# Dilated attention scores as two rounded 128-row products instead of one f32 product of 64 rows

## The chip, the cores and the metric

One core of one Trainium2 chip runs the whole program. Time is device microseconds of one execution; the figure for the kernel before is the median of three. The profile is of one further execution, and its times count from the start of its span.

## What is computed

Two transformer blocks over 512 tokens of width 1024, one after the other. The change is in the first block, in its dilated attention, cut here to what matters:

```python
def dilated_branch(q, k, v, rel_bias, window, dilation):
    ...
    s = jnp.einsum('bdhcqe,bdhcke->bdhcqk', qb, kb).astype(f32) + bias[:, None]
    s = jnp.where(mask, s, NEG)
    m = jnp.max(s, axis=-1, keepdims=True)
    p = jnp.exp(s - m)
    den = jnp.sum(p, axis=-1, keepdims=True)
    o = jnp.einsum('bdhcqk,bdhcke->bdhcqe', p, vb.astype(f32)) / den
    ...

def dilated_mixer(q, k, v, rel_bias):
    q = q * DSA_DH ** -0.5
    ...
    w = jax.nn.softmax(jnp.stack(lses, axis=0), axis=0)
    return jnp.sum(w[..., None] * jnp.stack(outs, axis=0), axis=0)

def first_block(x, ...):
    ...
    o_b = dilated_mixer(...).reshape(B, S, DSA_WIDTH)
    mixed = jnp.concatenate([o_a, o_b], axis=-1).astype(h.dtype)
    h = h + jnp.einsum('bsm,md->bsd', mixed, w_out[l])
```

There are 8 heads of 64 channels. The kernel folds the three dilations into one score matrix per head, with a table of biases (`toep`) that also counts how many dilations see a key, so each head needs one 512 x 512 causal score matrix.

## The kernel before, in words

Every large product is made of three rounded (fp32r) products: rounded part times rounded part, rest times rounded part, rounded part times rest. The three lines are L660, L664 and L667 (function `products`); a group of the three over 128 rows and 512 columns is called a triple below. The weights stream in on two DMA queues: SP loads raw pieces (`weights`, L2285), ScalarE rounds them (L1030) and writes the negated rounded part (L1038), and GpSimd's queue loads the same piece again, added onto that (L2187).

Each engine has one instruction list, written before the run by `merge`: every stream yields a due time before each step, and the step with the smallest due time is issued next. Due times set the order only; on the chip an engine runs its list in order and waits on semaphores. `T_A1` is the due time at which the product `wo0` (the first half of the output projection) starts, `R1` the due time between two steps of the dilated attention.

The dilated attention (`attention("dil", ...)` on TensorE, `dilated` on ScalarE and VectorE) runs in 12 steps beside the triples of `wo0`. A step s is a pair of heads `hp` (two heads, in partitions 0 to 63 and 64 to 127 of the pages `qD[hp]` and `kD[hp]`) and some rows of the score matrix; `ORDER` gives a pair three steps, of 384 columns, of 128 and 256 columns, and of 512 columns. One step goes through the engines like this:

- TensorE: the scores of both heads into banks `FB[0]` and `FB[1]`, in f32 with 64 rows per head (L858). This is called block S(s) below.
- VectorE: adds the bias and takes the row extreme (L1706), called the mask step; it frees the score bank for block S(s + 1).
- ScalarE: exponential with the row sum (L1152). VectorE: reciprocal (L1688) and scaling (L1693).
- TensorE, in step s + 2: transposes into `FB[2]`, `FB[3]` (L846), called T(s). ScalarE copies them out to `pT` (L1164).
- TensorE, in step s + 3: the values (L833), called AV(s), into bank `OB`. After a pair's third step VectorE copies `OB` out (L1676), which the next AV waits for.

```python
ORDER = [(hp, rows) for hp in range(4) for rows in (((2, 0),), ((0, 0), (1, P)), ((3, 0),))]
...
for i, at_ in rows_:
    n = (i + 1) * P
    for p in range(2):
        mm = e.matmul(FB[p][:, at_:at_ + n], qs[64 * p:64 * p + 64, hp, i * P:(i + 1) * P],
                      ks[64 * p:64 * p + 64, hp, 0:n], start=True, stop=True)
```

VectorE also adds finished tiles of `wo0` to the residual (L1755), and both engines split finished rows of `mixed` into rounded part (L1145) and rest (L1669).

Of the kernel before, what the change touches and what calls it, by code (L numbers as in the profile page):

```python
# [8 lines left out]
F32 = mybir.dt.float32  # L9
F32R = mybir.dt.float32r  # L10
U8 = mybir.dt.uint8
ALU = mybir.AluOpType
ACT = mybir.ActivationFunctionType

P = 128
# [255 lines left out]
def lo(x, k):  # L271
    return "operand_low", x, k
# [12 lines left out]
def build_program(nc, A, out):  # L285
    with ExitStack() as ctx:
# [20 lines left out]
        def rounded(name, n):  # L307

            return [nc.alloc_sbuf_tensor_at(f"{name}{i}_r", [P, S], F32R, offset=places[f"{name}{i}"])[:, :] for i in range(n)]
# [92 lines left out]
        AH2, AL2, ft2 = AH1_last, AL1_last, ft1  # L402
        sums2 = nc.alloc_sbuf_tensor_at("sums2", [P, 4 * UC], F32, offset=places["sq0"])[:, :]

        sq_r, gt_r, zb_r, eb_r = rounded("sq", 2), rounded("gT", 2), rounded("zb", 2), rounded("eb", 2)

        raw_r = nc.alloc_sbuf_tensor_at("RAW0_r", [P, 2 * S], F32R, offset=places["RAW0"])[:, :]
# [29 lines left out]
        def x_in(k):  # L437

            return [(f"x{k}",)]
# [5 lines left out]
        def freed(t):  # L445
            return ("evac_s" if t.st in on_act else "evac_v", t.g)
# [71 lines left out]
        def dil_done(hp):  # L518

            return T_A1 + R1 * (3 * hp + 5) + 0.9 if hp == 3 else T_A1 + R1 * (3 * hp + 6) + 1.3  # L520

        def row_stat(s, i, p):

# [92 lines left out]
        def tensor():  # L616
# [200 lines left out]
            def attention(name, T, R, q, apart, qs, ks, vs, zbuf, wbuf, q_key, k_key, v_keys, fence):  # L817
                for s in range(NA + 3):
# [29 lines left out]
                    if s < NA:  # L848
                        yield T + R * s + (2 * q if apart else q)
                        hp, rows_ = ORDER[s]  # L850
                        for p in range(2):
                            pe.wait_ge(q_key(hp), k_key(hp))
                            if s:
                                pe.wait_ge((name + "_b", s - 1, p))
# [5 lines that stand above are left out]
                                if (i, at_) == rows_[-1]:  # L860
                                    mm.then_inc(*pe.sig(name + "_z", s, p))
# [119 lines left out]
        def scalar():  # L981
# [160 lines left out]
            def mixed_split(st, k, time, waits):  # L1142
                yield time
                act.wait_ge(*waits)
                e.activation(NH[:, k, :], (mixed if st == "mixed" else mixed2)[:, k, :], ACT.Copy).then_inc(*act.sig(*hi(st, k)))  # L1145

            def exponentials(s):
                for p in range(2):
                    act.wait_ge(("dil_b", s, p))
                    for i, at_ in ORDER[s][1]:  # L1150
                        z, x = zs[2 * (s % 2) + p][:, at_:at_ + (i + 1) * P], row_stat(s, i, p)
                        ex = e.activation(z, z, ACT.Exp, scale=-1.0, bias=x[:, 0:1], accum_out=x[:, 2:3])  # L1152
                ex.then_inc(*act.sig("dil_e", s))
# [241 lines left out]
                return [up(t) if t.i % 2 else gate(t) for t in plan.stage["gu", g]]  # L1395

            streams = [prologue(), ones(), splits(), negated(), root("attn", mean_time["attn"]), columns("attn", 30.0)]
            streams += [natural("vG", vG, "attn"), natural("vD", vD, "attn")]
            streams += silu_gates("gG", lambda i: mixed[:, i, :], gt_, lambda i: [("gate", "gG", i - 2)] if i >= 2 else [])
            streams += [gla(0), gla(1)]  # L1400
            streams += [mixed_split("mixed", k, T_A1 - 2.0 + 0.2 * k, [("gla_out", k), ("product", "block", plan.last_unit("vD"), k)])
# [43 lines left out]
        def vector():  # L1445
# [220 lines left out]
            def mixed_split(st, k, time, waits):  # L1666
                yield time + 0.05
                dve.wait_ge(hi(st, k), *waits)
                e.tensor_tensor(NL[:, k, :], (mixed if st == "mixed" else mixed2)[:, k, :], NH[:, k, :].bitcast(F32),  # L1669
                                ALU.subtract).then_inc(*dve.sig(*lo(st, k)))  # L1670

            def heads_out(name, s, dst, last):
                hp = ORDER[s][0]
# [466 lines left out]
            streams += silu_gate("gG", lambda i: mixed[:, i, :], lambda i: g_gla[:, i:i + 1], gt_, [])  # L2140
            streams += [gla(0), gla(1), put("qD", qD, -0.125), put("kD", kD)]
            streams += [mixed_split("mixed", k, T_A1 - 2.0 + 0.2 * k, []) for k in range(4)]
            streams += [dilated(), to_h("wo0", "wo0", lambda k: x_in(k)[-1])]
            streams += [mixed_split("mixed", k, dil_done(k - 4), []) for k in range(4, 8)]
            streams += [to_h("wo1", "mlp", lambda k: ("h", "wo0", k)), sums("mlp")]
            streams += [operand_row("mlp", "n_mlp", k, square_time("mlp", k), g_mlp, [("h", "mlp", k)]) for k in range(4)]
# [118 lines left out]
        def sync():  # L2265
# [36 lines left out]
            def inputs():  # L2302
# [13 lines left out]
                yield 30.0  # L2316
                e.dma_start(cu_f, A["c_masks"]).then_inc(*sp.sig("masks_in", by=16))

            def toeplitz():
                for i, (h0, h1) in enumerate([(0, 1), (1, 3), (3, 5), (5, 8)]):  # L2320
                    yield gla_time(1, 12.5) if i < 2 else T_A1 - 0.9
                    sp.wait_ge(("band_stored",))
                    if i < 2:
                        sp.wait_ge(("gla_keep", 1, 0, 64), ("gla_keep", 1, 1, 64), ("gla_64", 1, 1), ("gla_diag", 1, 1))
                    else:
                        sp.wait_ge(("gla_end",))
                    src = bass.AP(tensor=band.ap().tensor, offset=2 * S * h0, ap=[[1, P], [2 * S, h1 - h0], [1, S]])
                    e.dma_start(toep[:, h0:h1, :], src).then_inc(*sp.sig(f"toep{i}", by=16))
# [14 lines left out]
                yield plan.end + 100  # L2343
                sp.wait_ge(("out", 8))

            yield from merge(weights(), quarter_weights(), inputs(), toeplitz(), outputs())

        for _ in merge(tensor(), scalar(), vector(), gpsimd(), sync()):
            pass
# [102 lines left out]
```

## Time and profile before

| | |
|---|---|
| median of 3 runs | 1357.74 us (1357.04 to 1358.72) |
| the profiled execution | 1356.61 us, span 1355.2 us |
| TensorE busy | 1345.9 us, 99% of the span |
| VectorE, ScalarE, GpSimd busy | 64%, 60%, 25% |
| granted TensorE clock | 1.0 of full speed in all 40 slices |
| the stage of the dilated attention | 172.2 to about 228 us, 12 steps |

Shares of busy time are averages over the whole span. Matmuls are pipelined, so what one costs TensorE is read from the distance between starts, not from its own duration. A row of a timeline merges equal instructions that follow each other; a number in brackets is the idle time before it and what ended that.

### The profile page before, as it was taken

Reading aid. Unit: us, or ns where it says so; the run is one execution under the profiler, and the core shown is the slowest. Engines: PE = TensorE matmul, PEld = TensorE weight load, DVE = VectorE, ACT = ScalarE, POOL = GpSimd, SP = SyncE. Lnnn points to the kernel's source line nnn. Section 1 sums busy time; section 2 is a strip of 40 time slices with the busy share of each in tenths; the row PEclk is TensorE's granted clock in tenths of the full one; section 3 lists DMA queues with packets and bytes.
Section 4 is the critical chain, followed back from the end, with each engine's and each line's share of the span. In section 5 each row is a group of like instructions: output and inputs, shape, how many; then the busy total and the mean of one; then the engine's idle time right before and its main releaser. Section 6 shows DMA issues by size and latency. Waiting matters only on the chain.

```text
span 1355.2 us, 19500 instructions
## 1 busy us (share of the span) xinstructions
PE 1345.9 (99%) x7510; PEld 1134.7 (84%) x7510; DVE 873.4 (64%) x1536; ACT 810.5 (60%) x1227; POOL 340.2 (25%) x314
## 2 busy tenths in 40 slices
PE   9999999999999999999999999999999999999999
PEld 6977967789899898887778888888888898889889
DVE  6055465577576672357798879965447785568557
ACT  6575556753544535666577777785656645753653
POOL 0211111235353251111211211211113161315214
PEclk9999999999999999999999999999999999999999
DMA  7975563925435138876655586767898546825723
GB/s 246 246 164 116 120 192 65 231 38 197 94 109 172 38 119 194 193 167 146 151 129 125 130 213 127 147 148 170 206 226 196 102 140 183 177 45 168 188 50 110
DMA packets 57969, 202.45 MB, mean 149 GB/s; under 512 B 6450, under 2 KB 7019, under 8 KB 57748
## 3 DMA queue, kind: packets, MB, share of 16 engines
q0 software_dynamic: 26784, 97.28, 38.0%
q1 hardware_dynamic: 30228, 102.04, 22.8%
q10 hardware_dynamic: 864, 1.87, 0.4%
q8 instruction: 60, 0.98, 0.3%
q14 instruction: 33, 0.27, 0.1%
HBM read 199.05 MB, written 2.12 MB: 148 GB/s over the span
## 4 chain that ended last, share of the span: by engine, by line
PE 83%; DVE 10%; ACT 4%; issue 2%; DMA 1%; SPq 0%; POOL 0%; DVEq 0%; ACTq 0%
PE bank L660 20%; PE bank L667 20%; PE bank L664 20%; PE bank L698 17%; DVE eb L1728 2%; PE bank L813 1%; DVE eb L1723 1%; PE bank L885 1%; PE bank L858 1%; DVE zb L1743 1%; DMA RAW<-in_w_in 1%; PE bank L833 1%; DVE zb L1731 1%; ACT WL L1038 1%; PE bank L846 1%
## 5 line engine op out<-in xcount | busy, mean ns | idle before, releaser
L660 PE MATMUL bank<-NH,WH 128*128 128x512 f32 x1152 | 459.4, 400 | 0.8 <-ACT NH L995 0.3
L664 PE MATMUL bank<-NL,WH 128*128 128x512 f32 x1152 | 448.1, 390 | 0.5 <-DVE NL L1470 0.5
L667 PE MATMUL bank<-NH,WL 128*128 128x512 f32 x1152 | 448.0, 390 | 0.4 <-DVE WL L1465 0.4
L660 PEld LDWEIGHTS bank<-NH,WH 128*128 128x128 f32 x1152 | 216.1, 188 | 61.1 <-issue 18.8
L667 PEld LDWEIGHTS bank<-NH,WL 128*128 128x128 f32 x1152 | 216.2, 188 | 47.0 <-DVE WL L1465 0.9
L664 PEld LDWEIGHTS bank<-NL,WH 128*128 128x128 f32 x1152 | 216.3, 188 | 45.0 <-DVE NL L1470 2.6
L1030 ACT ACTIVATE WH<-RAW 128x1024 fp32r<-128x1024 f32 (+3 forms) x140 | 143.5, 1030 | 72.2 <-PE bank L667 37.2
L698 PE MATMUL bank<-AH,WH 128*128 128x256 f32 x644 | 182.5, 283 | 0.3 <-DVE AL L2111 0.3
L698 PE MATMUL bank<-AL,WH 128*128 128x256 f32 x644 | 182.2, 283 | 0.0
L698 PE MATMUL bank<-AH,WL 128*128 128x256 f32 x644 | 182.2, 283 | 0.0
L1038 ACT ACTIVATE WL<-WH 128x1024 fp32r<-128x1024 f32 (+1 forms) x146 | 153.0, 1050 | 11.9 <-DMA WH<-in_w_in 9.7
L2187 POOL DMA_DIRECT2D WL<-in_w_in x58 | 50.8, 887 | 312.2 <-ACT WL L1038 302.5
L698 PEld LDWEIGHTS bank<-AH,WH 128*128 128x128 f32 x644 | 123.6, 192 | 0.9 <-ACT AH L1381 0.4
L698 PEld LDWEIGHTS bank<-AL,WH 128*128 128x128 f32 x644 | 123.6, 192 | 0.2
L698 PEld LDWEIGHTS bank<-AH,WL 128*128 128x128 f32 x644 | 123.6, 192 | 0.0
L2199 POOL TENSOR_TENSOR quarters<-quarters 128x512 f32<-128x512 f32 (+1 forms) x48 | 73.1, 1524 | 127.9 <-PE bank L667 59.7
L2199 POOL TENSOR_TENSOR quarters_s<-quarters 128x512 f32<-128x512 f32 (+1 forms) x48 | 78.2, 1629 | 96.9 <-PE bank L667 51.0
L1025 ACT ACTIVATE WH<-quarters 128x1024 fp32r<-128x1024 f32 (+3 forms) x72 | 62.4, 882 | 65.4 <-PE bank L698 45.0
L1815 DVE TENSOR_TENSOR WL<-quarters,WH 128x1024 fp32r<-128x1024 f32 (+3 forms) x72 | 85.1, 1183 | 7.1 <-ACT WH L1025 7.1
L1845 DVE TENSOR_TENSOR gains_hT<-gains_hT,bank 128x256 f32<-128x256 f32 x143 | 58.4, 414 | 17.1 <-PE bank L698 16.7
L660 PE MATMUL bank<-WH,NH 128*128 128x256 f32 (+2 forms) x224 | 67.3, 308 | 0.4 <-DVE kS L1897 0.3
L667 PE MATMUL bank<-WL,NH 128*128 128x256 f32 (+2 forms) x224 | 64.9, 299 | 0.0
(375 smaller groups left out, 2120.0 us busy)
## 6 DMA issues: line engine op xcount, KB each, us to landing
WL<-in_w_in POOLq DMA_DIRECT2D x58, 512.0 KB, 6.6
RAW<-in_w_gu SPq DMA_DIRECT2D x44, 512.0 KB, 5.3
WL<-in_w_gu POOLq DMA_DIRECT2D x34, 512.0 KB, 8.1
RAW<-in_w_ff SPq DMA_DIRECT2D x32, 512.0 KB, 4.9
WH<-in_w_in POOLq DMA_DIRECT2D x32, 512.0 KB, 6.7
RAW<-in_w_in SPq DMA_DIRECT2D x28, 512.0 KB, 6.0
quarters<-in_w_ff SPq DMA_DIRECT2D x24, 512.0 KB, 4.8
WL<-in_w_ff POOLq DMA_DIRECT2D x17, 512.0 KB, 6.5
```

The lines of the kernel that those rows point to most:

```text
L660: e.matmul(o, a[0], a[1], start=(k == 0), stop=False)
L664: e.matmul(o, b[0], b[1], start=False, stop=False)
L667: mm = e.matmul(o, c[0], c[1], start=False, stop=(k == t.kt - 1))
L698: mm = e.matmul(o, a, b, start=(n in OPENS and j == 0 and i == 0), stop=(n in CLOSES and j == pairs_ - 1 and i == 2), skip_group_check=True)
L1025: e.activation(WH[p % HL][:, 0:(c if k == 3 else 2 * c)], part, ACT.Copy).then_inc(*act.sig("high", p))
L1030: e.activation(WH[p % HL][:, 0:n], RAW[raw_slot[p]][:, 0:n], ACT.Copy).then_inc(*act.sig("high", p))
L1038: e.activation(WL[p % HL][:, 0:n], WH[p % HL][:, 0:n].bitcast(F32), ACT.Copy, scale=-1.0).then_inc(*act.sig("high_negated", p))
L1728: scan = e.tensor_tensor_scan(r, r, r, 0.0, ALU.add, ALU.max)
L1815: e.tensor_tensor(WL[(p + i) % HL][:, 0:n], x, WH[(p + i) % HL][:, 0:n].bitcast(F32), ALU.subtract).then_inc(*dve.sig("low_sum", p + i))
L1845: e.tensor_tensor(hT[:, row, ts], hT[:, row, ts], bank, ALU.add).then_inc(*dve.sig("h_part", u, n))
L2187: e.dma_start(WL[p % HL][:, 0:n], src[:, k * cols:(k + m) * cols], accum_op=ALU.add).then_inc(*pool.sig(f"low_added{p % HL}", p, by=16))
L2199: e.tensor_tensor(to, a, b, op).then_inc(*pool.sig("quarter_sum", u, key))
```

## The change

Before the scores of a head pair, ScalarE rounds q and k of both heads (two halves of 64 partitions each, 4 instructions), VectorE takes the rests (4 instructions), and SP's queue moves halves to the other 64 partitions by 6 DMAs from SBUF to SBUF, so that for each head a page of 128 rows holds the rounded part in one half and the rest in the other. A head's scores are then two fp32r products over 128 rows with the same stationary page: with the key page [rounded; rest] and with the page [rest; rounded]. The heads of a block no longer alternate: first head 0 (waiting only for its own mask step), then head 1.

Pages are memory that is free by then: for pair 0 pages of `mixed1` and the two `sq` pages, for pairs 1 and 3 the pages of qG, kG and vG (free at the end of the GLA part), for pair 2 pages of vG and those of pairs 0 and 1 of qD and kD.

```diff
+        late = [("qG", 0), ("qG", 1), ("kG", 0), ("kG", 1), ("vG", 0), ("vG", 1)]
+        stacks = [[page(*x) for x in pair] for pair in (
+            [("mixed1", 4), ("mixed1", 5), ("mixed1", 6), ("mixed1", 7), ("sq0", 0), ("sq1", 0)], late,
+            [("vG", 2), ("vG", 3), ("qD", 0), ("kD", 0), ("qD", 1), ("kD", 1)], late)]
+        q_rest = [page("qD", hp) for hp in range(4)]
...
+        def stack_time(hp, late_):
+            return T_A1 + (R1 * (3 * hp - 2 + late_) if hp else 4.0 * late_ - 28.0)
...
+                        if name == "dil":
+                            xa, xb, ya, yc, yb, yd = stacks[hp]
+                            pe.wait_ge(("dil_low", "q", hp), ("dil_low", "k", hp), ("stacked", hp))
+                            for p, x, ys in ((0, xa, (ya, yc)), (1, xb, (yb, yd))):
+                                if s:
+                                    pe.wait_ge(("dil_b", s - 1, p))
+                                for i, at_ in rows_:
+                                    n = (i + 1) * P
+                                    for y in ys:
+                                        mm = e.matmul(FB[p][:, at_:at_ + n], x[:, i * P:(i + 1) * P], y[:, 0:n],
+                                                      start=(y is ys[0]), stop=(y is ys[1]))
+                                mm.then_inc(*pe.sig("dil_z", s, p))
+                            continue
...
+            def stack_highs():
+                for hp in range(4):
+                    xa, xb, ya, yc, yb, yd = stacks[hp]
+                    back = [[("band_stored",)], [("gla_end",)], [("stacked", 0), ("stacked", 1), ("gla_end",)],
+                            [("dil_z", 5, 0), ("dil_z", 5, 1)]][hp]
+                    for n, (x, st, a, b) in enumerate((("k", "kD", ya, yb), ("q", "qD", xa, xb))):
+                        yield stack_time(hp, 0.25 + 0.05 * n)
+                        src = (qD if x == "q" else kD)[:, hp, :]
+                        act.wait_ge(freed(plan.stage[st][hp]), *back)
+                        e.activation(a[top_], src[top_], ACT.Copy)
+                        e.activation(b[bottom], src[bottom], ACT.Copy).then_inc(*act.sig("dil_high", x, hp))
...
+            def stack_lows():
+                for hp in range(4):
+                    xa, xb, ya, yc, yb, yd = stacks[hp]
+                    for n, (x, a, b, to_a, to_b) in enumerate((("k", ya, yb, yc, yd), ("q", xa, xb, q_rest[hp], q_rest[hp]))):
+                        yield stack_time(hp, 0.9 + 0.05 * n)
+                        src = (qD if x == "q" else kD)[:, hp, :]
+                        dve.wait_ge(("dil_high", x, hp))
+                        e.tensor_tensor(to_a[top_], src[top_], a[top_].bitcast(F32), ALU.subtract)
+                        e.tensor_tensor(to_b[bottom], src[bottom], b[bottom].bitcast(F32), ALU.subtract).then_inc(
+                            *dve.sig("dil_low", x, hp))
...
+            def stack_places():
+                for hp in range(4):
+                    xa, xb, ya, yc, yb, yd = stacks[hp]
+                    q_ = q_rest[hp]
+                    yield stack_time(hp, 0.92)
+                    sp.wait_ge(("dil_low", "k", hp))
+                    e.dma_start(ya[bottom].bitcast(F32), yc[top_].bitcast(F32)).then_inc(*sp.sig(f"stacked{hp}", "ya", by=16))
+                    e.dma_start(yc[bottom].bitcast(F32), ya[top_].bitcast(F32)).then_inc(*sp.sig(f"stacked{hp}", "yc", by=16))
+                    e.dma_start(yb[top_].bitcast(F32), yd[bottom].bitcast(F32)).then_inc(*sp.sig(f"stacked{hp}", "yb", by=16))
+                    e.dma_start(yd[top_].bitcast(F32), yb[bottom].bitcast(F32)).then_inc(*sp.sig(f"stacked{hp}", "yd", by=16))
+                    yield stack_time(hp, 0.97)
+                    sp.wait_ge(("dil_low", "q", hp))
+                    e.dma_start(xa[bottom].bitcast(F32), q_[top_].bitcast(F32)).then_inc(*sp.sig(f"stacked{hp}", "xa", by=16))
+                    e.dma_start(xb[top_].bitcast(F32), q_[bottom].bitcast(F32)).then_inc(*sp.sig(f"stacked{hp}", "xb", by=16))
+                    at["stacked", hp] = at[f"stacked{hp}", "xb"]
```

The streams `stack_highs()`, `stack_lows()` and `stack_places()` are added to those that `merge` orders on ScalarE, VectorE and SP. Where their steps come to stand:

ScalarE, steps 0 to 1 of the stage, before (zs are the scores after the mask step, pT the transposed weights):

```order
L1152 ACTIVATE zs_106,small<-zs_106,small 128x384
L1152 ACTIVATE zs_107,small<-zs_107,small 128x384
L1164 ACTIVATE pT_110<-bank 128x384
L1164 ACTIVATE pT_111<-bank 128x384
L1152 ACTIVATE zs_108,small<-zs_108,small 128x128
```

and now:

```order
L1196 ACTIVATE zs_106,small<-zs_106,small 128x384
L1196 ACTIVATE zs_107,small<-zs_107,small 128x384
L1188 ACTIVATE kG_page_177<-kD 64x512
L1189 ACTIVATE vG_page_179<-kD 64x512
L1188 ACTIVATE qG_page_175<-qD 64x512
L1189 ACTIVATE qG_page_176<-qD 64x512
L1208 ACTIVATE pT_110<-bank 128x384
L1208 ACTIVATE pT_111<-bank 128x384
```

The four roundings of pair 1 stand between the exponentials of step 0 and the copies of T(0). Those of pair 2 stand behind the copies of T(2), before L1038 and the copies of T(3), those of pair 3 between the copies of T(5) and of T(6), and those of pair 0 some 25 us before the stage.

VectorE, behind the mask step of step 1, before there came the reciprocal at once:

```order
L1706 ISA zs_109,small<-bank,toep 128x256
L1706 ISA small 128x1
L1688 RECIPROCAL small<-small 128x4
L1693 TENSOR_SCALAR zs_108<-zs_108,small 128x128
L1693 TENSOR_SCALAR zs_108<-zs_108,small 128x256
```

and now:

```order
L1761 ISA zs_109,small<-bank,toep 128x256
L1761 ISA small 128x1
L1723 TENSOR_TENSOR kG_page_178<-kD,kG_page_177 64x512
L1724 TENSOR_TENSOR vG_page_180<-kD,vG_page_179 64x512
L1723 TENSOR_TENSOR qD_page_185<-qD,qG_page_175 64x512
L1724 TENSOR_TENSOR qD_page_185<-qD,qG_page_176 64x512
L1743 RECIPROCAL small<-small 128x4
```

The rests of pairs 2 and 3 stand likewise behind the mask steps of steps 4 and 7, ahead of the copy of `OB` (pair 2) or of a residual add and that copy (pair 3).

SP's queue, behind the loads of the bias table, before there came the raw pieces of the next weights (in_w_ff):

```order
L2328 DMA toep<-band 128x3x512
L2285 DMA RAW_64<-in_w_ff 128x1024
L2285 DMA RAW_62<-in_w_ff 128x1024
L2285 DMA RAW_63<-in_w_ff 128x1024
L2285 DMA RAW_64<-in_w_ff 128x1024
```

and now (the six DMAs of pair 2 stand between the last two rows):

```order
L2399 DMA toep<-band 128x3x512
L2380 DMA kG_page_177<-kG_page_178 64x512
L2381 DMA kG_page_178<-kG_page_177 64x512
L2382 DMA vG_page_179<-vG_page_180 64x512
L2383 DMA vG_page_180<-vG_page_179 64x512
L2386 DMA qG_page_175<-qD_page_185 64x512
L2387 DMA qG_page_176<-qD_page_185 64x512
...
L2340 DMA RAW_64<-in_w_ff 128x1024
```

The first raw piece moves behind the DMAs of pairs 1 and 2, the second and third behind those of pair 3 as well.

## Rows read from the trace of the kernel before

**Rows 1.** The profile page, part 1: busy time and share of each engine.
```profile
PE 1345.9 (99%) x7510; PEld 1134.7 (84%) x7510; DVE 873.4 (64%) x1536; ACT 810.5 (60%) x1227; POOL 340.2 (25%) x314
```

**Rows 2.** The chain of waits, 165 to 250 us: start us, us, what.
```profile
195.02 0.49 ACT pT L1164
200.32 0.93 PE bank L858 x8
221.88 0.49 ACT pT L1164
```

**Rows 3.** Timeline of TensorE: start us, us, engine, line, form [idle before].
```profile
167.84 0.28 PE L667 MATMUL bank<-WL,NH 128*128 128x256 f32 x1
167.96 0.28 PE L660 MATMUL bank<-WH,NH 128*128 128x256 f32 x1
...
172.00 0.39 PE L667 MATMUL bank<-NH,WL 128*128 128x512 f32 x1
172.32 0.92 PE L858 MATMUL bank<-kD,qD 64*128 64x384 f32 x4
...
173.50 0.39 PE L664 MATMUL bank<-NL,WH 128*128 128x512 f32 x1
173.73 0.40 PE L667 MATMUL bank<-NH,WL 128*128 128x512 f32 x1
...
174.42 0.40 PE L667 MATMUL bank<-NH,WL 128*128 128x512 f32 x1
...
175.94 0.39 PE L664 MATMUL bank<-NL,WH 128*128 128x512 f32 x1
...
177.52 0.40 PE L667 MATMUL bank<-NH,WL 128*128 128x512 f32 x1
...
179.24 0.39 PE L664 MATMUL bank<-NL,WH 128*128 128x512 f32 x1
...
182.76 0.92 PE L858 MATMUL bank<-kD,qD 64*128 64x384 f32 x4 [0.59 <-DVE small L1706]
...
207.26 0.88 PE L833 MATMUL bank<-pT,vD 128*64 128x128 f32 x12
```

**Rows 4.** The same view, of a cut that ends inside block S(0).
```profile
172.32 0.59 PE L858 MATMUL bank<-kD,qD 64*128 64x384 f32 x2
```

**Rows 5.** The same view at f32 products of 128 columns, later in the kernel.
```profile
859.86 0.61 PE L885 MATMUL bank<-hX 128*128 128x128 f32 x4
860.23 0.48 PE L660 MATMUL bank<-NH,WH 128*128 128x512 f32 x1
```

**Rows 6.** Timeline of ScalarE.
```profile
168.53 2.31 ACT L1145 ACTIVATE NH<-mixed 128x512 fp32r<-128x512 f32 x4
...
176.93 0.87 ACT L1164 ACTIVATE pT<-bank 128x384 f32<-128x384 f32 x2 [1.65 <-PE bank L846]
...
190.38 0.87 ACT L1164 ACTIVATE pT<-bank 128x384 f32<-128x384 f32 x2 [1.97 <-PE bank L846]
...
204.39 0.87 ACT L1164 ACTIVATE pT<-bank 128x384 f32<-128x384 f32 x2 [2.38 <-PE bank L846]
```

**Rows 7.** Timeline of VectorE.
```profile
170.09 2.49 DVE L1669 TENSOR_TENSOR NL<-mixed,NH 128x512 fp32r<-128x512 f32 x4
...
179.57 0.18 DVE L1688 RECIPROCAL small<-small 128x4 f32<-128x4 f32 x1 [2.20 <-ACT zs L1152]
...
184.59 0.55 DVE L1706 CUSTOM_DVE_ANT_0 zs<-bank,toep 128x384 f32<-128x384 f32 x1
...
204.02 0.69 DVE L1676 COPY mixed<-bank 128x512 f32<-128x512 f32 x1 [0.29 <-PE bank L833]
```

**Rows 8.** One line's instructions: a VectorE operation of 16 partitions.
```profile
L1544 DVE COPY glT<-bank x1: 678/678/678, 50.6 to 50.6; 16x512 f32<-16x512 f32 x1
```

**Rows 9.** DMA issues of the whole span: KB each, median us from issue to landing.
```profile
out<-gains_hT SPq DMA_DIRECT2D x2, 128.0 KB, 1.7
toep<-band SPq DMA_DIRECT2D x2, 512.0 KB, 6.8
```

More of the change, by code:

```diff
@@ L403, in build_program, with page @@
         sums2 = nc.alloc_sbuf_tensor_at("sums2", [P, 4 * UC], F32, offset=places["sq0"])[:, :]
+        def page(name, i=0):
+            made = pages.get((name, i))
+            if made is None:
+                made = pages[name, i] = nc.alloc_sbuf_tensor_at(f"{name}_page{i}", [P, S], F32R, offset=places[name] + i * PAGE)[:, :]
+            return made
+        pages = {}
+        top_, bottom = slice(0, 64), slice(64, P)
+        late = [("qG", 0), ("qG", 1), ("kG", 0), ("kG", 1), ("vG", 0), ("vG", 1)]
[3 more added lines that the diff above has]
+        q_rest = [page("qD", hp) for hp in range(4)]
         sq_r, gt_r, zb_r, eb_r = rounded("sq", 2), rounded("gT", 2), rounded("zb", 2), rounded("eb", 2)
@@ L1397, in scalar @@
             streams = [prologue(), ones(), splits(), negated(), root("attn", mean_time["attn"]), columns("attn", 30.0)]
-            streams += [natural("vG", vG, "attn"), natural("vD", vD, "attn")]
+            streams += [natural("vG", vG, "attn"), natural("vD", vD, "attn"), stack_highs()]
             streams += silu_gates("gG", lambda i: mixed[:, i, :], gt_, lambda i: [("gate", "gG", i - 2)] if i >= 2 else [])
@@ L2142, in vector @@
             streams += [mixed_split("mixed", k, T_A1 - 2.0 + 0.2 * k, []) for k in range(4)]
-            streams += [dilated(), to_h("wo0", "wo0", lambda k: x_in(k)[-1])]
+            streams += [stack_lows(), dilated(), to_h("wo0", "wo0", lambda k: x_in(k)[-1])]
             streams += [mixed_split("mixed", k, dil_done(k - 4), []) for k in range(4, 8)]
@@ L2344, in outputs @@
                 sp.wait_ge(("out", 8))
-            yield from merge(weights(), quarter_weights(), inputs(), toeplitz(), outputs())
+            yield from merge(weights(), quarter_weights(), inputs(), toeplitz(), stack_places(), outputs())
         for _ in merge(tensor(), scalar(), vector(), gpsimd(), sync()):
```

## The prediction

> **What bounds the kernel now.** The page first: TensorE is busy 99% of the span [rows 1], so the whole is as long as its list of products and what that waits for. Then the chain of waits through the stage of the dilated attention [rows 2]: it runs on TensorE for stretches and twice crosses to the other engines, at the copies of transposed weights by ScalarE (195.02 and 221.88 are two of these crossings). From 200.32 to 221.5 it lies on TensorE alone. So a shorter score block is worth its full length only in the stretches where the chain is on TensorE; where it passes through ScalarE and VectorE, their lists set the pace. Last the timelines of the two [rows 6, 7]: their idle time shows how much work can be put in before they delay anything.
>
> **What a score block costs now.** Triples run at a distance of 0.23 us per product (173.50 to 173.73) [rows 3]. Block S(0) lies between the starts 172.00 and 173.50, where two distances of 0.23 would do: 1.50 - 0.46 = 1.04 us for 384 columns. In the same way S(1) (128 and 256 columns) costs 175.94 - 174.42 - 0.46 = 1.06 and S(2) (512 columns) 179.24 - 177.52 - 0.46 = 1.26 [rows 3]. Some 0.2 us of each are gaps: the block starts 0.09 late (172.32 for 172.23), and the product behind it keeps 0.34 from its successor instead of 0.23.
>
> **What it will cost.** Four rounded products over 128 rows, like those of the triples. Their distance is 0.23 at 512 columns and 0.12 at 256 (167.84 to 167.96) [rows 3], so by a straight line about 0.175 at 384. That gives 4 x 0.175 = 0.70 for the first block of a pair and 4 x 0.23 = 0.92 for the third. No row has a rounded product of 128 columns. Bounds: 0.065 by the straight line, or 0.19 as an f32 product of that width costs (four records, two products, in 859.86 to 860.23) [rows 5]. I take 0.12, the nearest measured distance of a rounded product with a fresh stationary operand: 4 x (0.12 + 0.12) = 0.96 (0.74 to 1.24). A pair then saves 0.34 + 0.10 + 0.34 = 0.78 us, the four pairs 3.1 us (2.0 to 4.0). The gaps go because no block changes between 64-row and 128-row products any more.
>
> A first rule is to be weighed here. The row shows that the two heads already run side by side: two records of 384 columns start together at 172.32 and take 0.59 [rows 4], and all four are through in 0.92 [rows 3], of which the last product's own run is a part; so the array time is not far above the 0.70 of the new form. The Trainium skill says the same in TensorE: Matmul & The Clock Gate, Part 3 on packing small matmuls: matmuls in different row groups run concurrently, and the gain of small contractions lies in that; stacking gives it up. By that page the array time would be nearly unchanged; TensorEngine Tiling, Key Properties, adds that changing the tiling mode drains the engine, which would be the gaps. By the first alone the saving is 0 (third rival), by both it is the 0.2 of a block.
>
> **What is added.** ScalarE: 16 roundings. Four of 128 x 512 follow each other in 2.31 [rows 6], 0.56 each; 64 partitions are taken at the same price, since on VectorE 16 partitions of 512 columns cost 0.68 [rows 8] and 128 cost the same (the copy of `OB`, 0.69) [rows 7]. So 2.25 us per pair. VectorE: 16 rests, four in 2.49 [rows 7], 0.60 each, 2.4 us per pair. SP: 24 DMAs of 128 KB. One of that size lands 1.7 us after issue alone, one of 512 KB in this stage 6.8 [rows 9]; I take 2 to 2.5 for the last of six, nearest to the row of equal size, as the queue is free by then: the three raw pieces (1.5 MB) that followed the bias table now wait behind these DMAs. That wait costs nothing: they are weights of the next stage, and the last of them is issued near 206.5, with some 20 us of this stage to come. GpSimd's queue is not passed.
>
> **Where it lies.** Pair 0 is prepared some 25 us ahead, in idle time of both engines. Cost 0.
>
> Pair 1. Both heads' scores were ready at 172.32 + 0.92 = 173.24 [rows 3]; the first head's two products now end near 172.75, so the mask step and the exponentials of step 0 come 0.5 earlier. ScalarE then rounds for 2.25, where it idled 1.65 before 176.93 [rows 6]: 1.65 + 0.5 - 2.25 = -0.1. The copies of T(0) come at their old time, and what S(0) and S(1) saved is gone. VectorE's 2.4 fit the idle 2.20 before 179.57 [rows 7] plus the 0.5. They begin 0.5 before 179.57 - 2.20 = 177.4 and end near 179.3; the last of the six DMAs is issued some 0.7 later, near 180.1 (estimate: two issues), and lands near 182.4. S(3) started at 182.76, after 0.59 of waiting for the second head's mask step [rows 3]; its first head now waits only for the first, so it could start near 182.2. The landing is a few tenths later, which delays nothing: the mask step behind it started only at 184.59 [rows 7].
>
> Pair 2. 2.25 against an idle 1.97 before 190.38 [rows 6]: the copies of T(3), and all the chain behind them, come 0.28 later. What S(3) to S(5) saved (0.78) is lost, since the chain crosses ScalarE again at 195.02 [rows 2].
>
> Pair 3. 2.25 against an idle 2.38 before 204.39 [rows 6]: fits. On VectorE the 2.4 stand ahead of the residual add and of the copy of `OB`, which ended at 204.7 [rows 7]. The add began at 204.02 - 0.29 - 0.60 = 203.1; now rests, add and copy end at 203.1 + 2.4 + 0.6 + 0.7 = 206.8. AV(6) waits for it; it started at 207.26 [rows 3]. So of what S(7) and S(8) gain, at most 0.2 to 0.4 passes this gate; I take 0.3.
>
> Behind it nothing is inserted, and the chain lies on TensorE up to 221.5 [rows 2]: S(9), S(10) and S(11) pay 0.34 + 0.10 + 0.34 = 0.78. The crossing at 221.88 then comes earlier by the same.
>
> **The sum**: 0.3 + 0.78 = 1.1 us less. The profiled execution took 1356.6, so 1355.5; it lay 1.1 under the median of the runs, which becomes 1357.7 - 1.1 = **1356.6**. With the bounds of the 128-column product (0.28 either way in S(10)) and with a gate at AV(6) between 0 and 0.8, the case by itself spans 1355.7 to 1357.3. That is under 0.1%, less than a measurement of this kernel can tell (0.2%, 2.7 us).
>
> **The rivals.**
>
> 1. *The whole saving arrives.* If all roundings and rests stay in idle time, each of the 12 blocks pays: 3.1 us, 1354.6, and up to 4.0, 1353.7. For it: the idle times of ScalarE before 176.93, 190.38 and 204.39 add to 6.0 [rows 6], against 6.75 put in. Against: they shrink as TensorE gets ahead. Chance 0.17.
>
> 2. *The halves land late, slower.* TensorE, in order, waits for the sixth DMA with all triples behind it. It decides from a landing about 3.9 us after issue: then S(3) starts at 184, and the mask step of 184.59 [rows 7] slips. At 6.8, the row of the bias table [rows 9], pairs 1 and 2 lose 2.9 each; those of pair 3 have no transfer of another stage ahead of them and are taken to land in time. 5.8 - 1.1 = 4.7 more: 1362.4. Against: the queue is emptier than for those 6.8. The Trainium skill, SBUF — State Buffer, "Can I just issue two DMAs to hit both halves?" and the table before it, says that 64 partitions use 8 of 16 ports (some 218 GB/s); by an estimate from it the six take 3.6 us in a row and the last lands near 183.9, still under the deciding point. No row here shows such a copy. Chance 0.13.
>
> 3. *No gain.* If the products of a block, whose first stationary page cannot be loaded before the wait ends, keep a gap of 0.2, a pair saves 0.14 - 0.10 + 0.14 = 0.18, and the 0.28 of pair 2 eats what arrives: about 1357.9. For it: the near-equal array time above. Chance 0.12.
>
> That the change does not do what it says is excluded: TensorE's list has four 128-row products where two of 64 rows stood.
>
> **How the numbers follow.** Forecast 0.58, rivals 0.17, 0.13 and 0.12. Faster by over 0.2% (under 1355.0): rival 1 and a small edge of the forecast, 0.19. Slower by over 0.2% (over 1360.5): rival 2, 0.13. Within: 0.68. The range leaves out most of rival 2 and the edge of rival 1: 1354.3 to 1358.9.
>
> **What would show it.** Right: blocks of 0.70, 0.92 to 1.0 and 0.92 with no 0.34 behind them; 0.56 per rounding and 0.60 per rest; landings near 182.4; ScalarE without idle time before the copies of T(0) and T(3); AV(6) released by the copy of `OB`; about 1 us gained between 204 and 222. Wrong: idle TensorE before S(3) or S(6) released by DMA (rival 2); the chain on TensorE through the whole stage (rival 1); blocks near 0.9 and 1.1 (rival 3).

## The result and the profile after

The changed kernel takes 1363.47 us (median of 5 runs, 1362.02 to 1365.73) against 1357.04 for the kernel before on the same chip (5 runs): ratio 1.0049 with the interval 1.0034 to 1.0064, so slower by about half a per cent. Forecast was 1356.6, range 1354.3 to 1358.9: **wrong**, and on the other side. The profiled execution took 1362.78, its span 1361.5.

TensorE's busy time did not move, though a block needs less of it (it answers to [rows 1]; the page counts 99% either way):

```profile
PE 1345.4 (99%) x7510; PEld 1141.6 (84%) x7510; DVE 885.2 (65%) x1552; ACT 821.1 (60%) x1243; POOL 339.8 (25%) x314
```

What TensorE waited for between 130 and 235 us (the view of its waits: total us, times, longest):

```profile
PE bank L879 <- issue: 4.6, 1, 4.6
PE bank L865 <- DVE zs L1748: 2.0, 4, 1.0
PE bank L879 <- DMA qG_page<-qD_page: 1.7, 1, 1.7
```

L879 is the new score block. It waits twice, 6.3 us together, about the whole loss. The chain of waits (start us, us, what) shows both places:

```profile
177.20 0.60 DVE kG_page L1723
177.81 0.70 DVE vG_page L1724
...
181.59 2.91 DMA qG_page<-qD_page
184.59 0.93 PE bank L879 x4
...
197.33 4.55 issue
201.88 1.06 PE bank L879 x4
202.94 0.43 PE bank L679
```

First, S(3) at 184.59 is released by the landing of pair 1's sixth half. Second, S(6) starts at 201.88 after 4.55 us for which the view names no releaser. SP's list and the landings of that stretch name it: the sixth half of pair 2 is issued at 194.93, and of its line's four DMAs one landed 6.9 us after issue, which puts it at 201.83. The landings of that line, then SP's timeline (start us, us):

```profile
DMA to landing us min/median/max: 2.3/4.0/6.9
```
```profile
178.52 0.47 SPq L2380 DMA_DIRECT2D kG_page<-kG_page  x1
179.03 0.60 SPq L2381 DMA_DIRECT2D kG_page<-kG_page  x1
...
181.59 0.60 SPq L2387 DMA_DIRECT2D qG_page<-qD_page  x1
191.77 0.46 SPq L2380 DMA_DIRECT2D qD_page<-kD_page  x1
...
194.93 2.76 SPq L2387 DMA_DIRECT2D vG_page<-qD_page  x1
197.73 0.59 SPq L2340 DMA_DIRECT2D RAW<-in_w_ff  x1
```

Six issues take 3.7 us (178.52 to 182.19), and one took 2.76. The DMA issues of 191 to 203 us (KB each, median us to landing) show what else was on the way: pair 2's halves share the engines with three transfers of 512 KB. `WL` starts first, at 192.57; `WH` (197.63) and `RAW` (197.73) start only behind the issue of the sixth half.

```profile
WL<-in_w_out POOLq DMA_DIRECT2D x1, 512.0 KB, 8.1
WH<-in_w_out POOLq DMA_DIRECT2D x1, 512.0 KB, 7.5
RAW<-in_w_ff SPq DMA_DIRECT2D x1, 512.0 KB, 7.5
qD_page<-kD_page SPq DMA_DIRECT2D x2, 128.0 KB, 3.7
kD_page<-qD_page SPq DMA_DIRECT2D x2, 128.0 KB, 4.1
vG_page<-qD_page SPq DMA_DIRECT2D x2, 128.0 KB, 6.3
```

The `WL` piece is the one to look at. ScalarE has pair 2's four roundings ahead of the piece's negation (L1070), so GpSimd starts its accumulating DMA later. ScalarE after, then GpSimd after, then GpSimd before:

```profile
188.62 0.62 ACT L1188 ACTIVATE qD_page<-kD 64x512 fp32r<-64x512 f32 x1
...
191.21 1.06 ACT L1070 ACTIVATE WL<-WH 128x1024 fp32r<-128x1024 f32 x1
```
```profile
192.57 0.87 POOL L2242 DMA_DIRECT2D WL<-in_w_out  x1 [10.09 <-ACT WL L1070]
```
```profile
188.71 0.87 POOL L2187 DMA_DIRECT2D WL<-in_w_out  x1 [7.04 <-ACT WL L1038]
```

The negation stands 3.86 later than before: 2.6 of that are the four roundings ahead of it, the rest is that the stage already lay behind (the copies of T(2) start at 187.65, before at 186.40). By an estimate from these rows, without the roundings the piece would have had a head start of some 1.8 us on the first half (191.77); now it starts between the second and the third, ahead of the last four.

A third loss follows from the second. By the table of stretches (columns: length, then busy us and counts of PE, PEld, DVE, ACT, POOL, then PEclk, DMA share, GB/s) the granted clock, 1.00 up to 200, is 0.82 and 0.76 in the next two stretches:

```profile
200.00:204.00 4.00, 2.12 (x7) 1.89 (x8) 1.91 (x6) 0.90 (x3) 0.00 (x0) 0.82 0.73 247
204.00:208.00 4.00, 4.00 (x30) 3.07 (x29) 0.92 (x3) 1.25 (x4) 0.55 (x1) 0.76 0.25 48
```
```profile
202.73 0.63 PE L679 MATMUL bank<-NH,WH 128*128 128x512 f32 x1
203.16 0.63 PE L683 MATMUL bank<-NL,WH 128*128 128x512 f32 x1
```

TensorE had stood still for 4.55 us; behind that, products are 0.43 apart instead of 0.23, the lower of its two levels, 1.2 GHz. The chain gives the six products from 202.94 to 205.50 as 2.56 us instead of 1.38: 1.2 us more.

The blocks themselves came as forecast. TensorE's timeline of the first two:

```profile
172.32 0.39 PE L686 MATMUL bank<-NH,WL 128*128 128x512 f32 x1
172.54 0.51 PE L879 MATMUL bank<-mixed_page,mixed_page 128*128 128x384 f32 x2
...
173.49 0.40 PE L683 MATMUL bank<-NL,WH 128*128 128x512 f32 x1
...
174.41 0.39 PE L686 MATMUL bank<-NH,WL 128*128 128x512 f32 x1
174.64 0.62 PE L879 MATMUL bank<-mixed_page,mixed_page 128*128 128x128 f32 x4
...
175.80 0.40 PE L683 MATMUL bank<-NL,WH 128*128 128x512 f32 x1
```

By the prediction's own rule: 173.49 - 172.32 - 0.46 = 0.71 and 175.80 - 174.41 - 0.46 = 0.93 (forecast 0.70 and 0.96); S(2) gave 0.92. The blocks of a pair cost 2.56 for 3.36.

### The profile page after: what moved, and what is told of

Read it like the earlier page. It is cut to its first block, busy times and chain, and to the rows that moved or that the text cites. A ratio compares the mean times of both kernels' runs of the same rounds, so it can differ in the third digit from the quotient of the medians.

```text
span 1361.5 us, 19552 instructions
## 1 busy us (share of the span) xinstructions
PE 1345.4 (99%) x7510; PEld 1141.6 (84%) x7510; DVE 885.2 (65%) x1552; ACT 821.1 (60%) x1243; POOL 339.8 (25%) x314
## 4 chain that ended last, share of the span: by engine, by line
PE 89%; DVE 3%; ACT 3%; DMA 2%; issue 1%; SPq 0%; POOL 0%; ACTq 0%; POOLq 0%
PE bank L679 22%; PE bank L686 22%; PE bank L683 21%; PE bank L717 16%; PE bank L832 1%; PE bank L865 1%; PE bank L852 1%; PE bank L917 1%; DMA WL<-in_w_in 1%; PE bank L890 1%; ACT zs L1196 1%; DMA RAW<-in_w_in 1%; ACT WH L1062 1%; DVE zb L981 0%; DVE eb L975 0%
## 5 line engine op out<-in xcount | busy, mean ns | idle before, releaser
L1070 ACT ACTIVATE WL<-WH 128x1024 fp32r<-128x1024 f32 (+1 forms) x146 | 153.0, 1050 | 11.0 <-DMA WH<-in_w_in 8.8
```

The source lines that it names most:

```text
L1070: e.activation(WL[p % HL][:, 0:n], WH[p % HL][:, 0:n].bitcast(F32), ACT.Copy, scale=-1.0).then_inc(*act.sig("high_negated", p))
```

## The experiments

The totals of one kernel spread over 2.4 to 4.6 us on one chip (the kernel before: 1355.31 to 1360.95 in all runs), and the start of the stage moves by 1.4 us between profiles (171.87 to 173.27 for S(0)). So the stage is measured in itself: from the first product of S(0) to the first of the last AV, and in parts by the starts of S(3), S(6) and S(9), all from TensorE's timelines, in us. Each part comes from one profile; where two kernels do the same work (before and pair0 from S(3) on) the parts agree to 0.02. The last columns are the median of a kernel's runs and its ratio to the runs of the kernel before on the same chip, with the interval. By these intervals only the change, two_queues, direct and direct_idle differ from the kernel before; what is said of the others is read from the stage.

| kernel | S(0)-S(3) | S(3)-S(6) | S(6)-S(9) | S(9)-AV(11) | stage | median | ratio |
|---|---|---|---|---|---|---|---|
| before | 10.44 | 12.85 | 14.01 | 17.32 | 54.62 | 1357.04 | |
| the change | 12.05 | 17.29 | 14.69 | 17.25 | 61.28 | 1363.47 | 1.0049 (1.0034 to 1.0064) |
| weights_after | 11.58 | 13.65 | 13.53 | 16.90 | 55.66 | 1357.40 | 1.0002 (0.9993 to 1.0012) |
| early2 | 12.11 | 12.31 | 14.60 | 16.89 | 55.91 | 1357.18 | 1.0001 (0.9992 to 1.0011) |
| two_queues | 12.04 | 14.73 | 13.46 | 16.93 | 57.16 | 1359.31 | 1.0021 (1.0011 to 1.0030) |
| half_rows | 10.50 | 13.84 | 14.16 | 17.20 | 55.70 | 1357.61 | 1.0007 (0.9998 to 1.0017) |
| saving_only | 9.27 | 12.85 | 13.58 | 17.15 | 52.85 | 1355.89 | 0.9993 (0.9984 to 1.0002) |
| work_only | 11.42 | 13.34 | 14.13 | 17.34 | 56.23 | 1358.36 | 1.0008 (0.9999 to 1.0017) |
| pair0 | 10.09 | 12.85 | 13.99 | 17.33 | 54.26 | 1356.40 | 0.9995 (0.9986 to 1.0005) |
| direct | 11.88 | 14.93 | 15.59 | 19.54 | 61.94 | 1363.89 | 1.0049 (1.0034 to 1.0064) |
| direct_idle | 11.88 | 14.91 | 15.59 | 19.54 | 61.92 | 1364.65 | 1.0052 (1.0040 to 1.0065) |
| direct_zero | 10.67 | 14.47 | 14.27 | 17.24 | 56.65 | 1357.87 | 1.0004 (0.9995 to 1.0013) |
| three64 | 10.04 | 13.44 | 13.81 | 17.44 | 54.73 | 1356.72 | 0.9996 (0.9987 to 1.0005) |

**1. No transfers (half_rows).** Is it the landing, or the work ahead of it?

```diff
-pe.wait_ge(("dil_low", "q", hp), ("dil_low", "k", hp), ("stacked", hp))
+pe.wait_ge(("dil_low", "q", hp), ("dil_low", "k", hp))
-mm = e.matmul(FB[p][:, at_:at_ + n], x[:, i * P:(i + 1) * P], y[:, 0:n], ...)
+mm = e.matmul(FB[p][:, at_:at_ + n], x[r_, i * P:(i + 1) * P], y[r_, 0:n], ...)
```

> Leaves out the 24 placements; each product of the stacked scores runs over the 64 rows that a head's own half holds (same columns, same number of products, other numbers). Roundings and rests stay. Theory A (the stage is late because the sixth half lands late): the waits of 1.69 us before S(3) and of 4.55 us before S(6) go, the clock stays up, and the time is that of the kernel before less the shorter blocks, 1355.5 to 1357.5. Rival C (the 5.4 us of roundings and rests in a pair make the chain late, the landing only shows it): the waits are renamed, PE waits for ScalarE or VectorE in their place, and the time stays over 1360.

Measured: stage 55.70, 5.6 below the change, and 1357.61, at the upper end of A's range and far from rival C's 1360. So the landing carries the loss (A), but not all: the stage is still 1.08 over the kernel before although the blocks are shorter. TensorE now waits for the other engines, as rival C said, only for less (the view of its waits, 165 to 235 us; the second row is the copy of `OB`, and its 0.8 us stand at AV(6), the gate that the prediction priced):

```profile
PE bank L865 <- DVE zs L1748: 2.5, 3, 1.2
PE bank L852 <- DVE mixed L1731: 1.2, 2, 0.8
```

**2. Two queues (two_queues).** Does SP's issue make the sixth half late? `yb`, `yd` and `xb` go to GpSimd's queue.

```diff
-e.dma_start(yb[top_]..., yd[bottom]...).then_inc(*sp.sig(f"stacked{hp}", "yb", by=16))
+e.dma_start(yb[top_]..., yd[bottom]...).then_inc(*pool.sig(f"stackedpool{hp}", "yb", by=16))
...
```

> All work as in the changed kernel, but head b's three halves of a pair are issued by GpSimd, head a's three by SP. Theory A1 (SP issues one DMA of 64 partitions in 0.60 to 0.64 us, so the sixth is issued 3.1 us after the first): the last issue of pair 1 moves from 181.59 to some 180.0, lands near 182.6, the 1.69 us wait falls to under 0.5; pair 2's last is issued near 194 and lands by 199, its wait falls from 4.55 to some 2; time 1358 to 1360. Rival B (the transfers themselves are limited, by the ports of 64 partitions or by the engines that carry the weights): the sixth half lands when it does now, waits of 1.5 to 2 and 4 to 5, time 1362 to 1364.

Measured: in pair 1 the last issue moved to 179.73, 1.3 earlier than the 181.04 of early2, whose stage started within 0.07 of this one, and S(3) began at the same moment, 184.10 in both. Issued earlier, the halves took longer (3.9 and 4.1 us for the last two, 2.7 in early2). The last issues on SP and on GpSimd, then the view of 172 to 190 us: the rate in 40 equal slices of 0.45 us, and the landings:

```profile
179.46 0.46 SPq L2397 DMA_DIRECT2D qG_page<-qD_page  x1
```
```profile
179.73 0.52 POOL L2321 DMA_DIRECT2D qG_page<-qD_page  x1 [0.35 <-DVE qD_page L1724]
```
```profile
GB/s 259 314 391 382 382 355 369 382 423 369 378 387 387 255 91 73 209 305 278 305 273 291 68 64 91 164 127 91 228 191 191 64 0 0 0 0 0 0 0 0
...
qG_page<-qD_page SPq DMA_DIRECT2D x1, 128.0 KB, 3.9
qG_page<-qD_page POOLq DMA_DIRECT2D x1, 128.0 KB, 4.1
```

So for pair 1 A1 falls and B's wait stands (1.67): an issue 1.3 earlier brings no earlier landing. In the change six of 128 KB, 0.64 us apart, are some 205 GB/s. The Trainium skill, SBUF — State Buffer, Door 1: The DMA port swizzle, has 64 partitions reach 8 of 16 ports and some 218 GB/s. The 205 lie close to it, but they are also no more than SP's pace, 0.60 an issue and 0.04 between, and from two queues the six moved at 273 to 305 GB/s (179.65 to 181.9), so the six together are not held to it. What holds the last half in pair 1 stays open. Pair 2's wait fell to 1.99 and the time to 1359.31, both as A1 had said; but there GpSimd's halves also stand ahead of the weight piece in its own queue (192.96 and 193.47), so this run does not part the two causes for pair 2, which led to experiment 4.

**3. Earlier (early2).** Pair 2 one pass earlier.

```diff
-return T_A1 + (R1 * (3 * hp - 2 + late_) if hp else 4.0 * late_ - 28.0)
+return T_A1 + (R1 * (3 * hp - 2 + late_ - (0, 0, 1, 0)[hp]) if hp else 4.0 * late_ - 28.0)
```

> Pair 2's roundings, rests and placements stand one pass earlier; pairs 0, 1 and 3 as in the changed kernel. Theory A with lead time: pair 2's halves land by about 192 to 194, before S(6) needs them near 197; the wait of 4.55 goes and with it the half clock after it, while S(3)'s 1.69 stays: time 1357.3 to 1358.8. Rival C (the added ScalarE and VectorE work binds wherever it stands): the chain from scores to weights is late by the same 2.5 to 2.8 us one pass earlier, time over 1360.

Measured: stage 55.91, time 1357.18; S(6) waits for nothing, the clock stays at 1.00, and rival C (over 1360) falls. The same six DMAs now run ahead of the weight piece (issued at 190.23, beside the sixth at 190.29) and land in 2.3 to 2.7 us (medians) instead of 3.7 to 6.3. S(6) to S(9) is 0.59 longer than before, with a wait of 0.99 at AV(6) for the copy of `OB`, the prediction's gate; in the change nothing waits there. DMA issues of 186 to 200 us:

```profile
qD_page<-kD_page SPq DMA_DIRECT2D x2, 128.0 KB, 2.3
kD_page<-qD_page SPq DMA_DIRECT2D x2, 128.0 KB, 2.3
vG_page<-qD_page SPq DMA_DIRECT2D x2, 128.0 KB, 2.7
```

**4. Only the weight pieces moved (weights_after).** The sharpest test: the change as it is, with two added waits on GpSimd (pieces 31 and 32 are those that it starts at 181.60 and 192.57 in the change).

```diff
-pool.wait_ge(("high_negated", p))
+pool.wait_ge(("high_negated", p), *{31: [("stacked", 1)], 32: [("stacked", 2)]}.get(p, []))
```

> The changed kernel, but GpSimd starts the two weight pieces that it added at 181.60 and 192.57 (512 KB each) only when pair 1's and pair 2's placements have landed; nothing else moves. Theory B (pair 2's halves landed 3.7 to 6.9 us after issue because the piece's transfer was ahead of them; the same six landed in 2.3 to 2.7 where the engines were free): pair 2's sixth half lands near 197.4, S(6)'s wait falls from 4.55 to 0 to 0.8, the clock does not fall, pair 1's wait from 1.69 to 1.1 to 1.5; time 1357.5 to 1359.5. Rival A1 (SP's issue, 2.76 us for the sixth, is itself the delay, or the raw piece behind it): pair 2's sixth still lands 6 to 7 us after issue, a wait of over 3.5, time over 1361. A second rival: the pieces come too late for their own products, and PE waits for them in place of the halves by 1 to 4 us.

Measured: the stage is 55.66, 5.62 shorter, and the time that of the kernel before, 0.1 under theory B's range. Pair 2's halves land in 2.3 to 3.0, SP issues the sixth in 0.60 instead of 2.76, S(6) waits 0.90 (0 to 0.8 was expected) and the clock stays at 1.00. GpSimd's piece, released by the landing; the landings of 190 to 203 us; and S(3) and S(6):

```profile
197.99 1.09 POOL L2242 DMA_DIRECT2D WL<-in_w_out  x1 [12.64 <-DMA vG_page<-qD_page]
```
```profile
vG_page<-qD_page SPq DMA_DIRECT2D x2, 128.0 KB, 3.0
```
```profile
183.90 0.59 PE L879 MATMUL bank<-kG_page,qG_page 128*128 128x384 f32 x2 [1.21 <-DMA qG_page<-qD_page]
...
197.55 0.41 PE L879 MATMUL bank<-qD_page,vG_page 128*128 128x384 f32 x1 [0.90 <-issue]
```

Theory B is shown for pair 2: the long issue was a result of the loaded engines, not a cause. No product waited for the pieces, which came 2.8 and 5.4 us later. For pair 1 only 0.5 of the 1.7 was the piece (S(3) waits 1.21); the rest is there without it, with halves that take 2.5 to 2.8 us behind rests that end at 179.9 in the change.

**5. Saving alone, work alone.** What is the change worth without the transfers? In saving_only `qf` and `kf` are rows of `NH`, and nothing is prepared; in work_only the old f32 blocks run beside all roundings and rests.

```diff
 saving_only
-mm = e.matmul(..., x[:, i * P:(i + 1) * P], y[:, 0:n], ...)
+mm = e.matmul(..., qf[r_, i * P:(i + 1) * P], kf[r_, 0:n], ...)
 work_only
-if name == "dil":
+if name == "none":
```

> No roundings, no rests, no placements: every score block is two fp32r products over 64 rows of a tile that holds something else (other numbers, the same count of products and columns). The stage from the first product of S(0) to the last AV took 54.62 us in the kernel before. If the blocks' 0.78 in a pair reaches the end in all four pairs, the stage is 51.5 long and the time 1354.0. If most of it is lost in the waits for VectorE and ScalarE, as pair 0 alone showed (its stage 54.26, so 0.36), four pairs give 0.4 to 1.4: 1355.6 to 1356.7.

> Roundings and rests of all four pairs where the changed kernel has them, into pages that nothing reads; no placements; the scores are the products of the kernel before. Theory C2 (the added work is late for the chain by about what half_rows showed, 1.08 over the kernel before, and the shorter blocks give back a part): the stage is 1.5 to 2.5 us over 54.62 and the time 1358.6 to 1359.6. Rival (the work lies in idle time and only shortens it): the stage within 0.4 of 54.62, time 1356.8 to 1357.5; then half_rows' 1.08 came from the products.

Measured: with no preparation at all the blocks of a pair cost 2.49 (0.75, 0.87, 0.87), 3.5 us less in four pairs, and the stage is 1.77 shorter: **half of the saving arrives**, 1.17 of it before S(3), nothing between S(3) and S(6) (12.85 as before), 0.43 up to S(9) and 0.17 behind it. Work alone costs 1.61 in the stage, as theory C2 said; the rival's "idle time" falls. Both together (half_rows) are 1.08 over the kernel before, not 1.61 - 1.77 = -0.16. That fits shorter blocks which shrink the idle time that the work was to fill, but no run shows this by itself.

**6. One pair (pair0).** Only the pair that is prepared 20 us ahead.

```diff
-if name == "dil":
+if name == "dil" and hp in (0,):
-for hp in range(4):
+for hp in (0,):
```

> Only pair 0 (S(0) to S(2)) takes the stacked products; pairs 1 to 3 take the products of the kernel before, with none of their roundings, rests or placements. If the saving of 0.78 us in a pair's three blocks reaches the end: 1356.0 to 1356.6. If it is lost in the next wait of S(3) or S(4), or eaten by the 0.3 us by which the stage began later in the changed kernel: 1356.9 to 1357.4. The start of the stage tells whether pair 0's preparation (147 to 153 us) is what made it 0.32 late: 171.16 then, 170.84 if not.

Measured: stage 54.26, 0.36 of the 0.78 arrives, the rest is lost before S(3), where TensorE waits 0.66 for the mask step as before [rows 3]. The stage began at 172.89 here, and at 172.69 in saving_only, which prepares nothing, against 172.32 before: the later start scatters between profiles and says nothing about pair 0's preparation. The best of the stacked forms, but its ratio does not leave 1.

**7. No transfers, all terms (direct, direct_idle, direct_zero, three64).** VectorE can write a rest into the other half of a page itself, and GpSimd can double a half, so no DMA is needed. In direct and direct_idle the second product has 64 rows; in direct_zero it has 128, half of them zero; three64 has no stacking.

```diff
 direct, direct_idle
+e.matmul(FB[p][...], x[:, ...], y[:, 0:n], start=True, stop=False)
+e.matmul(FB[p][...], x[r_, ...], yc[r_, 0:n], start=False, stop=True)
+e.tensor_tensor(xa[bottom], src[top_], xa[top_].bitcast(F32), ALU.subtract)
+e.tensor_copy(ya[bottom], ya[top_].bitcast(F32))
 direct_zero
+e.matmul(FB[p][...], x[:, ...], z[:, 0:n], start=False, stop=True)
+e.memset(yc[bottom].bitcast(F32), 0.0)
 three64
+for j, (x, y) in enumerate(((xa, ya), (xa, yc), (xb, ya))):
+    e.matmul(FB[p][...], x[r_, ...], y[r_, 0:n], start=(j == 0), stop=(j == 2))
```

> No placements by DMA: the queries' rests are written by VectorE straight into the other half of the page, the keys' rounded halves are doubled by two GpSimd copies a pair, and the second product takes 64 rows (rounded queries by keys' rests); the product of the two rests, below rounding, is left out. Roundings and rests stand where the changed kernel has them, so ScalarE and VectorE carry the same. If the lateness was the transfer's alone: S(3) and S(6) wait for no landing, stage 55.3 to 56.1, time 1357.2 to 1358.2, as without placements. If the copies of GpSimd (1.1 to 1.7 us for 128 rows in the rows of its sums) come as late as the DMAs: a wait before S(3) of over 1 us and a time over 1359.

> As the one without DMA placements, but the roundings stand in ScalarE's idle stretches of the kernel before (before exp of S(0), S(3) and S(6), and two others) and the rests of pairs 2 and 3 and pair 1's queries on GpSimd. If the added work on ScalarE and VectorE was what ate the shorter blocks: the stage comes near the one with the saving alone, 53.2 to 54.2, time 1355.6 to 1356.6, below the kernel before. If GpSimd's 1.6 us an operation makes pair 1 late (9 us of work from 173 on): a wait of 0.5 to 2 us before S(3) and no gain, 1357 to 1358.5.

Both missed, by about 6 us, for a reason that neither theory had (direct's time is over the 1359 of its rival, but without the wait that was to make it). Nothing waits (at most 0.6 us in the whole stage); the blocks are long. direct_idle's block S(0):

```profile
172.42 0.39 PE L686 MATMUL bank<-NH,WL 128*128 128x512 f32 x1
172.65 0.33 PE L878 MATMUL bank<-mixed_page,mixed_page 128*128 128x384 f32 x1
172.91 0.43 PE L879 MATMUL bank<-mixed_page,mixed_page 64*128 64x384 f32 x1
173.27 0.44 PE L878 MATMUL bank<-sq_page,mixed_page 128*128 128x384 f32 x1
```

A 128-row and a 64-row product in turn are 0.26 to 0.37 apart where two alike are 0.17; a pair's blocks cost 1.46 + 2.28 + 1.72 = 5.46 us. That led to the other two.

> No placements by DMA; VectorE writes the queries' rests into the other half of their page, GpSimd doubles the keys' rounded halves, and the second product runs over all 128 rows, its other half cleared to zero by GpSimd (the product of the two rests is left out). Roundings in ScalarE's idle stretches, rests in VectorE's idle stretches, the queries' rests of pairs 1 and 2 on GpSimd. Theory D (in the two runs before, the change between products of 128 and of 64 rows made the blocks long: 0.36 us from product to product for 384 columns against 0.17): the blocks fall from 1.44, 2.25 and 1.68 to the changed kernel's 0.7 to 1.1, and with no landing to wait for and the work in idle time the stage is 53.2 to 54.4 against 54.62 before, time 1355.6 to 1356.9: below both kernels. If instead the writes of GpSimd or across the halves made the products slow: blocks and time as in the two runs before, 1363 to 1365. If the added work still binds: 54.6 to 56, 1357 to 1358.5.

> No stacking at all: the rounded part and the rest of a pair's queries and keys stand in four full pages (one rounding and one rest of 128 rows each, half as many operations), and a head's scores are three products of 64 rows: rounded by rounded, rounded by rest, rest by rounded. In the run with half rows the 64-row products of the two heads ran side by side, 0.28 a product of 384 columns for both heads and 0.34 of 512. If that holds, the blocks cost some 0.92, 1.1 and 1.1, 0.24 a pair below the kernel before, and with half the added work the stage is 54.0 to 54.8, time 1356.4 to 1357.4, well below the changed kernel. If a third product breaks the side-by-side run: blocks of 1.2 to 1.6, stage over 55.5, time over 1358.

direct_zero: with 128 rows the products are 0.17 to 0.18 apart again (theory D shown), but the stage is 56.65: TensorE waits 3.1 us for VectorE's scaling, and behind the longest of these waits the granted clock is 0.57 from 196 to 200. The nine products from 196.58 to 199.95 take 3.37 us where full clock makes 1.85 (five at 0.23, four at 0.175), so 1.5 us go to the clock. Why VectorE is late is seen beside GpSimd's subtractions (last section). The hoped-for gain did not come.

```profile
194.84 0.55 PE L865 MATMUL bank<-cf,zs 128*128 128x128 f32 x3 [1.38 <-DVE zs L1755]
```

three64: its S(1) costs 1.37 for the 1.1 that was expected and the pair 3.38, so it saves nothing on TensorE; with half the added work the stage is 54.73 and the time that of the kernel before, both as expected. No version was found that beats both kernels by a measurable margin.

## Why the prediction was wrong

- **Block cost: right.** 0.71, 0.93, 0.92 against 0.70, 0.96, 0.92, without the gaps. That two heads side by side would leave no saving (third rival) is refuted.
- **Price of the work: too low.** 64 partitions cost 0.64 a rounding (175.01, 175.64, 176.29 on ScalarE) and 0.70 a rest (177.11 to 177.81 on VectorE) where 0.56 and 0.60 were taken: 2.6 and 2.8 per pair instead of 2.25 and 2.4. A single operation of 128 partitions lasts as long (0.62 on ScalarE, 0.69 on VectorE); what is gone is the overlap of one with the next, which [rows 6] and [rows 7] had in their merged rows. Why it is gone was not tested.
- **"The last of six issued some 0.7 later, near 180.1": wrong.** Six issues at 0.64 put it at 181.59, and it landed at 184.5, not 182.4: 2.9 us behind its issue where 2 to 2.5 were taken. In two_queues an issue 1.3 earlier brought no earlier landing.
- **Pair 2: the step that failed.** It counted ScalarE's 0.28, which the sum then left out, and no transfer at all, on the word that "GpSimd's queue is not passed". The list was not passed, but the time was: the roundings, and the 1.25 by which the stage already lay behind, moved the negation from 187.35 to 191.21, and with it 512 KB of weights from 188.71 to 192.57, among the halves. Price: 4.44 between S(3) and S(6) and some 1.2 of clock behind it, a term that the prediction had nowhere. weights_after, which moves only the pieces, gets back 3.64 of the 4.44 and 1.16 behind S(6); the 0.80 that stay are not the piece's. (Its other 0.82 come before S(3) and behind S(9).) early2 gets back 5.4, but moves pair 2's work as well.
- **"S(9), S(10) and S(11) pay 0.78": wrong.** In the change S(9) to AV(11) gained 0.07, in the undisturbed early2 and weights_after 0.43 and 0.42, and with no work at all 0.17. That the chain lies on TensorE there [rows 2] does not mean that a shorter block pays in full: the other engines' steps stand just behind it. In saving_only TensorE waits 0.30 for ScalarE's copies in this part, where the kernel before has no wait for them.
- **Rival 2 was right in mechanism and nearly in time** (1362.4 for 1363.47), by other terms: pair 1 lost 1.6 and pair 2 4.4 where 2.9 each was written, and the clock came on top; that its time lies so near is luck. Its deciding point, a landing 3.9 us after issue, was passed by issuing late in pair 1 (2.9 us) and by 6.9 us in pair 2. Its chance of 0.13 leant on "the queue is emptier", which looked at SP's queue and not at the engines both queues share.

The account, change less before, in the parts of the table: 1.61 + 4.44 + 0.68 - 0.07 = 6.66; the medians differ by 6.43.

## What to carry to other kernels

When work is put in front of an instruction that releases a DMA, place that DMA anew and ask whom it now meets: a transfer that nobody waited for can start a few microseconds later into one that TensorE waits for. If two transfers collide and only one is urgent, a wait on the other queue is enough (5.6 us for two waits here). And ask what a shorter block is worth with no cost at all before pricing its preparation: here 1.8 of 3.5 us, hardly more than the 1.6 that the work alone cost.

## What the hardware showed beyond that

- **Rows in turn.** Products of 128 and 64 rows in turn are 0.26 to 0.37 apart at 384 columns, two of 128 rows 0.17. In the rows of weight loads the loads at each change (172.91, 173.27, 173.64) start with their products instead of ahead of them. The Trainium skill, TensorEngine Tiling (Array Packing), Key Properties, says that changing the tiling mode drains TensorE; the trace agrees, and a change costs 0.09 to 0.20 us here.
- **GpSimd beside VectorE.** The scaling of two tiles of 128 x 384 takes 0.75 us alone, as all through three64, where GpSimd subtracts nothing, and 1.71 or 2.25 while GpSimd subtracts; the rest of 64 x 512, 0.69 elsewhere, took 1.69. VectorE in direct_idle, then in direct_zero:

```profile
175.96 1.71 DVE L1754 TENSOR_SCALAR zs<-zs,small 128x384 f32<-128x384 f32 x2
...
189.16 2.25 DVE L1754 TENSOR_SCALAR zs<-zs,small 128x384 f32<-128x384 f32 x2
```
```profile
177.94 1.69 DVE L1723 TENSOR_TENSOR vG_page<-kD,vG_page 64x512 fp32r<-64x512 f32 x1
```

- **A DMA's issue can be a wait.** SP's row of 2.76 us shrank to 0.60 when the weights were kept away (weights_after).
- **The clock.** It fell behind a wait of 4.55 us in the change and behind 1.38 and 0.30 in direct_zero, and stayed at 1.00 behind 1.99 in two_queues: the length of the last wait alone does not tell.
